# A long fp32 network, 256 tokens by 1024 features, on one core: another order at its beginning, at three boundaries and at its end, with GpSimd as a fourth arithmetic engine at the beginning

## The reference

```
def first_block(x, c, ctx, c_ctx, ...):        # sh, sc, ga = parts of silu(c) @ w_mod + b_mod
    hc = rmsnorm(ctx, g_mix) * (1 + csc1) + csh1
    hx = rmsnorm(x, g_mix) * (1 + sc1) + sh1
    x = x + ga1 * mlstm_mixer(hx, hc, ...)     # two directions, 4 heads, context as first state
    hx = rmsnorm(x, g_ffn) * (1 + sc2) + sh2
    x = x + ga2 * conv_glu(hx, ...)            # 1024 -> 2*2816 -> 1024
    return rmsnorm(x, g_final)

def sublayer(x, shift, scale, gate, g_pre, g_post, fn, w):
    h = rmsnorm(x, g_pre) * (1 + scale) + shift
    return x + w * gate * rmsnorm(fn(h), g_post)

def second_block(x, c, ...):                   # mods = silu(c) @ cond_w + cond_b
    x = sublayer(x, ..., swiglu_1, 0.5)        # stage f1
    x = sublayer(x, ..., gla_mixer, 1.0)       # stage gla, 4 heads
    x = sublayer(x, ..., swiglu_2, 0.5)        # stage f2
    k, v = mla_shared_kv(rmsnorm(x, kv_g) * (1 + kv_scale) + kv_shift)
    x = sublayer(x, ..., swiglu_3, 0.5)        # stage f3
    x = sublayer(x, ..., mla_mixer, 1.0)       # stage mla, 8 heads, causal softmax
    return sublayer(x, ..., swiglu_4, 0.5)     # stage f4
```

## Time and profile before

| | |
|---|---|
| three executions | 1379.90, 1382.67, 1385.39 us |
| their median | 1382.67 us |
| the profiled execution | 1383.82 us, of which 1382.0 us from its first to its last instruction |
| TensorE busy | 1354.5 us (98%) |
| DVE busy | 1121.2 us (81%) |
| ACT busy | 785.7 us (57%) |
| GpSimd busy | 1.4 us |
| DMA read | 335.5 MB, 244 GB/s over the span |

### The profile page before, as it was taken

The page is one execution under the profiler, slowest core; times in us unless marked ns, Lnnn a source line. Parts: engine busy times, 40 slices in busy tenths (PEclk is TensorE's granted clock), DMA queues, the critical chain, the costliest instruction groups (busy, mean ns, idle before and its releaser), DMA issues.

```text
span 1382.0 us, 19144 instructions
## 1 busy us (share of the span) xinstructions
PE 1354.5 (98%) x7488; PEld 1164.1 (84%) x7488; DVE 1121.2 (81%) x1652; ACT 785.7 (57%) x1153; POOL 1.4 (0%) x6
## 2 busy tenths in 40 slices
PE   7999999999999999999999999999999999999998
PEld 4988987888878888889878888888888998888886
DVE  7787787998988998779788888889888797796653
ACT  7623657666456555474475555476554646755552
POOL 0000000000000000000000000000000000000000
PEclk9999999999999999999999999999999999999999
DMA  9657445775958888767449778768879561575551
GB/s 379 264 197 281 152 138 182 279 259 198 332 201 305 303 278 320 288 244 271 154 175 328 284 281 327 278 246 319 294 288 379 197 226 64 199 259 183 183 187 57
DMA packets 63001, 337.77 MB, mean 244 GB/s; under 512 B 6960, under 2 KB 9392, under 8 KB 34752
## 3 DMA queue, kind: packets, MB, share of 16 engines
q1 hardware_dynamic: 62448, 335.35, 66.7%
q0 software_dynamic: 288, 1.05, 0.2%
q10 hardware_dynamic: 176, 0.16, 0.0%
HBM read 335.49 MB, written 1.05 MB: 244 GB/s over the span
## 4 chain that ended last, share of the span: by engine, by line
PE 89%; DVE 4%; ACT 3%; DMA 2%; issue 1%; SPq 0%; ACTq 0%; DVEq 0%
PE bank L313 87%; DMA XF<-xT 1%; DMA raw<-w_stream 1%; ACT rstd L665 1%; ACT T L760 1%; DVE wlo L309 1%; DVE X L854 1%; PE bank L635 1%; ACT whi L291 1%; PE bank L912 0%; DVE SGC L835 0%; PE bank L1042 0%; DVE XN L795 0%; PE bank L2370 0%; DVE wlo L282 0%
## 5 line engine op out<-in xcount | busy, mean ns | idle before, releaser
L313 PE MATMUL bank<-hh,whi 128*128 128x512 f32 (+1 forms) x2160 | 661.6, 369 | 4.0 <-DVE hh L558 3.4
L313 PE MATMUL bank<-hh,wlo 128*128 128x256 f32 x1896 | 525.7, 280 | 0.0
L309 DVE TENSOR_TENSOR wlo<-raw,whi 128x2048 fp32r<-128x2048 f32 x199 | 454.4, 2286 | 40.4 <-ACT whi L291 40.1
L313 PEld LDWEIGHTS bank<-hh,whi 128*128 128x128 f32 x2160 | 387.2, 190 | 79.7 <-DVE wlo L309 3.3
L291 ACT ACTIVATE whi<-raw 128x2048 fp32r<-128x2048 f32 x198 | 378.3, 1915 | 118.2 <-PE bank L313 84.5
L313 PEld LDWEIGHTS bank<-hh,wlo 128*128 128x128 f32 x1896 | 356.7, 189 | 0.0
L313 PE MATMUL bank<-whi,hid_hi 128*128 128x512 f32 x440 | 172.2, 391 | 0.0
L313 PE MATMUL bank<-whi,hid_lo 128*128 128x512 f32 x440 | 171.4, 390 | 0.0
L313 PE MATMUL bank<-wlo,hid_hi 128*128 128x512 f32 x440 | 171.3, 389 | 0.0
L937 DVE SCALAR_TENSOR_TENSOR mring<-mring,con 128x1024 f32<-128x1024 f32 x107 | 130.2, 1219 | 14.1 <-DMA mring<-m_stream 14.0
L1123 ACT ACTIVATE GU<-bank 128x512 f32<-128x512 f32 x100 | 59.1, 591 | 109.3 <-PE bank L313 109.3
(11 more groups left out here) (327 smaller groups left out, 1428.1 us busy)
## 6 DMA issues: line engine op xcount, KB each, us to landing
raw<-w_stream SPq DMA_DIRECT2D x217, 1024.0 KB, 5.1
mring<-m_stream SPq DMA_DIRECT2D x139, 512.0 KB, 5.0
cb<-m_stream SPq DMA_DIRECT2D x53, 512.0 KB, 5.2
raw<-w_stream SPq DMA_DIRECT2D x4, 512.0 KB, 7.3
con<-const_d SPq DMA_DIRECT2D x1, 1472.0 KB, 15.1
XF<-xT SPq DMA_DIRECT2D x1, 1024.0 KB, 13.2
XC<-ctxT SPq DMA_DIRECT2D x1, 1024.0 KB, 10.2
y<-OUT SPq DMA_DIRECT2D x4, 256.0 KB, 2.6
```

Of the source, the lines that this page charges most:

```text
L309: nc.vector.tensor_tensor(w_lo(c, 0, CW), raw[:, c % RAW_SLOTS], w_hi(c, 0, CW).bitcast(f32), ALU.subtract).then_inc(s_lo, 1)
L313: return nc.tensor.matmul(out, lhsT, rhs, start=start, stop=True, skip_group_check=True)
```

## The change

The change has five parts.

1. **Beginning.** DVE makes only the rest of the first half of chunk 8; GpSimd makes the second half's and both halves of chunk 9's (`pool_rest`, counted by `s_plo`, "first_rests_by_pool"), and then sums ACT's eight context squares in pairs (`pool_context_pairs`), so that the mean square is 2 float32 matmuls in place of 8. These stand between the two halves of keys(0,0). `pe_first_chunks` takes the products in another order. ACT splits chunk 9 in halves, one before the input tiles and one behind the second of them, and rounds chunks 10 and 11 before it squares the context.
2. **Turned tiles.** For t = 0 the tiles 4 and 5 go to bank 5 in place of bank 6, except at f3 and mla; only tile 6 waits.
3. **GLA.** SP issues chunk 92 ahead of the modulation rows; DVE takes a modulation row earlier, and the bias and coefficients of f2 before the last head.
4. **MLA.** Twelve matmuls of the output projection go before the last head's transposes and before its values.
5. **End.** For t = 1 TensorE turns the old X by 8 float32 matmuls with the identity, among the last output products, and adds the stage's output times the diagonal of rstd by 8 more (`pe_add_out`); ACT makes that diagonal, and the two updates of DVE are gone.

```diff
+        def dve_half_rest(dve, c, half):
+            units_ahead[c] = units[0]
+            a = half * HALF
+            dve.wait_ge((s_hih, s_hi)[half], c + 1)
+            nc.vector.tensor_tensor(w_lo(c, a, a + HALF), raw[:, c % RAW_SLOTS, a:a + HALF],
+                                    w_hi(c, a, a + HALF).bitcast(f32), ALU.subtract).then_inc((s_loh, s_lo)[half], 1)
...
+        s_plo = sem("first_rests_by_pool")
+        def pool_rest(pool, c, half):
+            a = half * HALF
+            pool.wait_ge((s_hih, s_hi)[half], c + 1)
+            nc.gpsimd.tensor_tensor(w_lo(c, a, a + HALF), raw[:, c % RAW_SLOTS, a:a + HALF],
+                                    w_hi(c, a, a + HALF).bitcast(f32), ALU.subtract).then_inc(s_plo, 1)
+        def pool_context_pairs(pool):
+            for n, j in enumerate((0, 4)):
+                pool.wait_ge(s_sq, DT + j + 4)
+                nc.gpsimd.tensor_tensor(SQF[:, j:j + 2], SQF[:, j:j + 2], SQF[:, j + 2:j + 4], ALU.add)\
+                    .then_inc(s_cpair, 1)
+            pool.wait_ge(s_cpair, 2)
+            nc.gpsimd.tensor_tensor(SQF[:, 0:2], SQF[:, 0:2], SQF[:, 4:6], ALU.add).then_inc(s_cpair, 1)
+        def pe_context_stat(pe):
+            pe.wait_ge(s_cpair, 3)
+            for j in range(2):
+                ins = mm(bank[7][:, SEQ:], ones, SQF[:, j], j == 0)
+            ins.then_inc(s_stat, 1)
         def pe_first_chunks(pe, u0, c):
...
+            def out(n, m):
+                return bank[4 + n][:, m * SEQ:(m + 1) * SEQ]
+            def high(k, n, m):
+                w = w_hi(c + n, (m * DT + k) * P, (m * DT + k + 1) * P)
+                mm(out(n, m), w, hhi[:, k], k == 0 and m == 0)
+                mm(out(n, m), w, hlo[:, k], False)
+            def low(k, n, m):
+                return mm(out(n, m), w_lo(c + n, (m * DT + k) * P, (m * DT + k + 1) * P), hhi[:, k], False)
             pe.wait_ge(s_hi, c + 1)
+            pe.wait_ge(s_loh, c + 1)
             for k in range(DT + 2):
                 if k < DT:
                     pe.wait_ge(s_h, u0 + k + 1)
-                    high(k, 0)
+                    high(k, 0, 0)
+                    low(k, 0, 0)
+                    high(k, 0, 1)
                 if k == 2:
-                    pe.wait_ge(s_hi, c + 2)
+                    pe.wait_ge(s_hih, c + 2)
                 if k >= 2:
...
+                    high(k - 2, 1, 0)
+            pe.wait_ge(s_hi, c + 2)
+            pe.wait_ge(s_plo, 2)
+            for k in range(DT):
+                high(k, 1, 1)
+                ins = low(k, 0, 1)
+                low(k, 1, 0)
+            ins.then_inc(s_pe, 1)
+            pe.wait_ge(s_plo, 3)
+            for k in range(DT):
+                ins = low(k, 1, 1)
+            ins.then_inc(s_pe, 1)
...
+        KEPT = ("f3", "mla")
+        def turned(pre, t, j):
+            b, n = (j // 2, j % 2) if t else (((6, 7, 6, 7) if pre in KEPT else (6, 7, 5, 6))[j // 2],
+                                              j // 4 * 2 + j % 2)
...
-                    if t == 0 and j == 4:
+                    if t == 0 and j == (4 if pre in KEPT else 6):
                         pe.wait_ge(s_t, MODULATED[pre] + 1)
-                    if t == 0 and j == 6:
+                    if t == 0 and j == 6 and pre in KEPT:
                         pe.wait_ge(s_vt, PRES.index(pre) + 1)
-                    nc.tensor.transpose(turned(t, j), XN[:, j * P:(j + 1) * P], ident).then_inc(s_tpn, 1)
+                    nc.tensor.transpose(turned(pre, t, j), XN[:, j * P:(j + 1) * P], ident).then_inc(s_tpn, 1)
...
+        s_dg = sem("last_rstd_diagonal")
+        def turned_out(t, j):
+            return bank[(6, 4)[t] + j // 4][:, (j % 4) * P:(j % 4 + 1) * P]
         def pe_turn_out(pe, t):
+            for j in range(DT):
+                if t == 0 and j % 4 == 0:
+                    pe.wait_ge(s_xu, XU["f4"] + j // 4 + 1)
+                if t == 0:
+                    nc.tensor.transpose(turned_out(t, j), X[:, t, j * P:(j + 1) * P], ident).then_inc(s_tpn, 1)
+                else:
+                    mm(turned_out(t, j), X[:, t, j * P:(j + 1) * P], ident, j % 4 == 0)
+        def pe_add_out(pe):
+            pe.wait_ge(s_dg, 1)
             for j in range(DT):
                 if j % 4 == 0:
-                    pe.wait_ge(s_xu, XU["f4"] + 2 * t + j // 4 + 1)
-                nc.tensor.transpose(bank[(6, 4)[t] + j // 4][:, (j % 4) * P:(j % 4 + 1) * P],
-                                    X[:, t, j * P:(j + 1) * P], ident).then_inc(s_tpn, 1)
+                    pe.wait_ge(s_tw, 4 * STAGES.index("f4") + 3 + j // 4)
+                mm(turned_out(1, j), TW[:, j // 4, (j % 4) * P:(j % 4 + 1) * P], XN[:, 0:P], False).then_inc(s_tpn, 1)
...
                 elif t:
+                    n = rn("post", "f4", 1)
+                    act.wait_ge(s_rr, n + 1)
+                    nc.scalar.activation(XN[:, 0:P], ident, ACT.Copy, scale=rr[:, n:n + 1]).then_inc(s_dg, 1)
                     act_turned_out(act, 1)
...
-                else:
+                elif t == 0 or stage != "f4":
                     dve_update(dve, stage, t)
...
-                pe_out_last(pe, c0 + FT + last, 2 * last, hid_hi, hid_lo, mid=lambda: pe_turn_out(pe, 0))
-                pe_turn_out(pe, 1)
+                pe_out_last(pe, c0 + FT + last, 2 * last, hid_hi, hid_lo, mid=lambda: pe_turn_out(pe, 0),
+                            second=lambda: pe_turn_out(pe, 1))
+                pe_add_out(pe)
...
-                pe_pair(pe, c + 3 + j, 4 + a % 3, *(((hhi, hlo), (chi, clo))[n]), n == 1)
+                pe_pair(pe, c + 3 + j, 4 + a % 3, *(((hhi, hlo), (chi, clo))[n]), n == 1,
+                        between=(lambda: pe_context_stat(pe)) if a == 2 else None)
...
+            dve_half_rest(dve, c, 0)
...
-            nc.vector.tensor_tensor(modc[:], pm[:, 1], cols[:, 0:FIRST_MODS], ALU.add)
             link(dve, nc.vector.tensor_tensor(mod[:, 0:FIRST_MODS], pm[:, 0], cols[:, 0:FIRST_MODS], ALU.add))
             dve_coef_pre(dve, 1, 8, col("g_mix", 0, 8))
             dve_modulate(dve, N_X1, cq(1), mcol(0), "x1", XF)
-            dve_split(dve, c)
-            dve_split(dve, c + 1)
+            link(dve, nc.vector.tensor_tensor(modc[:], pm[:, 1], cols[:, 0:FIRST_MODS], ALU.add))
             dve_coef_pre(dve, 0, 8, col("g_mix", 0, 8), modc)
-            dve_split(dve, c + 2)
+            dve_split(dve, c + 2, 3)
             dve_split(dve, c + 3)
...
             dve_split(dve, c + 14)
-            mods(dve, 2)
+            mods(dve, 3)
...
-            finish_head(3)
-            dve_split(dve, c + 16)
-            mods(dve, 1)
-            for j in range(17, 19):
-                dve_split(dve, c + j)
             bias(dve, "gla")
             dve_pre_coef(dve, "f2")
+            finish_head(3)
+            for j in range(16, 19):
+                dve_split(dve, c + j)
             dve_boundary(dve, "gla")
...
+            def out_first(g, t):
+                for half in range(2):
+                    if t == 0 and g == 0:
+                        pe.wait_ge(s_h, U["mla_y"] + 7 + half)
+                    ins = mm3w(out_bank(t, half), c, g * D + half * 512, tok(hhi, g, t), tok(hlo, g, t), g == 0)
+                return ins
...
+                    pe.wait_ge(s_lo, c + 1)
+                    pe.wait_ge(s_h, U["mla_y"] + 6)
+                    out_first(0, 1)
                 transposes(h)
                 if 0 < h < MLA_HEADS - 1:
                     values(h - 1)
+            out_first(1, 1)
             values(MLA_HEADS - 1)
...
+                ins = out_first(g, 0)
             ins.then_inc(s_pe, 1)
...
-                    if c in EARLY and c not in (C_GLA, C_FFN[2], C_KV + 1):
+                    if c in EARLY and c not in (C_FFN[2], C_KV + 1):
                         continue
...
-            pool.wait_ge(s_lo, C_LSTM + 1)
+            pool.wait_ge(s_hi, C_LSTM + 1)
             pool.dma_start(cb[:], c_row.partition_broadcast(P)).then_inc(s_in[4], 16)
+            pool_rest(pool, C_LSTM, 1)
+            for half in range(2):
+                pool_rest(pool, C_LSTM + 1, half)
+            pool_context_pairs(pool)
```

More of the change, by code:

```diff
@@ L274, in act_second_half @@
             nc.scalar.activation(w_hi(c, HALF, CW), raw[:, c % RAW_SLOTS, HALF:], ACT.Copy).then_inc(s_hi, 1)
[L276 to L283 removed]
+        def dve_half_rest(dve, c, half):
[4 more added lines that the diff above has]
+                                    w_hi(c, a, a + HALF).bitcast(f32), ALU.subtract).then_inc((s_loh, s_lo)[half], 1)
+        def dve_halves(dve, c):
+            for half in range(2):
+                dve_half_rest(dve, c, half)
         def act_split(act, c):
@@ L1304, in pe_lstm @@
             pe.wait_ge(s_mm0, 1)
-            pe_stat(pe, N_CTX)
             def keys(j, n):
```

40 lines of the change are left out of this document (8 added, 32 removed).

## The result

| | before | after |
|---|---|---|
| median | 1383.97 us (5 runs) | 1395.80 us (5 runs) |
| lowest and highest | 1379.90, 1385.61 | 1391.30, 1396.05 |
| profiled execution | 1383.82 us, span 1382.0 | 1395.80 us, span 1394.0 |

The ratio is 1.0075, 95% interval 1.0057 to 1.0094, so the change costs 10.4 us (7.9 to 13.0). I had forecast 1382.6 in a range of 1378.5 to 1389, with 0.11 on slower by more than 0.5%.

What follows compares the result with a forecast made beforehand. It took TensorE, busy 98% of the span, as the bound; -1.95 - 0.95 - 0.60 + 0.2 + 3.2 = -0.1 on 1383.82 gave 1383.7, or 1382.6 in the median's terms, range 1378.5 to 1389.

Steps and rivals of the forecast that it cites:

- GpSimd's rests are hidden: Beginning: GpSimd's half rests, 2.3 us each from about 34.2, and its sums end in time, with 2 us to spare.
- keys(1,0) -1.95: Beginning: keys(1,0) starts at 69.0 in place of 70.96 us, behind a new wait of 1.6.
- the first rival: Beginning: DVE and GpSimd take turns reading SBUF; keys(1,0) +1.15 for -1.95, time 1385.7 us; chance 0.36.
- The forecast's other half: Beginning: 16.2 us of DVE and ACT work from the mean square's end to keys(1,0), no instruction changed.
- GpSimd starts late: Beginning: GpSimd's first operation may be late; free up to 5.6 us, at 8 us costs 2.4 (1385.0); chance 0.12.
- Turned tiles, 0: Boundaries of f0 and f1: the first wait goes, the second grows by as much; gain 0.
- GLA, -0.95: gla's boundary: chunk 92's load goes ahead of two modulation rows, lands about 2 us earlier, removing TensorE's 0.95 wait.
- f2's -0.60: f2's boundary: a modulation unit done earlier, in an idle of DVE, removes TensorE's idle of 0.60 us.
- MLA, +0.2 (up to +1.2): MLA's last head: 0.99 of waits go, 0.8 and some 0.4 come; +0.2 us, between -0.9 and +1.2.
- The end, +3.2 with +1.4 as the other end: Last products: eight added turns cost 1.8 us; diagonal products at half clock give +3.2, at full clock +1.4.

Runs made afterwards that it cites:

- e9: Kernel before, with GpSimd adding spare SBUF tiles 48 times in stage f1, work that nothing needs; f1 is 36 us longer.
- e3: Kernel before with the changed beginning alone, GpSimd filling its three half rests with zeros (writes only); ratio 0.9994.
- e10: Kernel before with the changed beginning alone, GpSimd's three rests waiting for the end of DVE's scaling; ratio 1.0023.
- e1: Kernel before with the change's beginning (part 1) alone; ratio 1.0058.
- experiment 10: Kernel before with the GLA part alone, one execution; f2's boundary -0.8, gla's load 5.0 us with no wait.
- e8: Kernel before with e7's beginning, turned tiles, GLA part, old end, and only three MLA output products moved; median 1380.31 us, ratio 0.9971.
- e7: Kernel before with the changed beginning alone, DVE making the half rests and square sums in GpSimd's place; ratio 0.9992.

## Why the prediction was wrong, step by step

- **The step that failed: GpSimd's rests are hidden.** The forecast gave keys(1,0) -1.95; it is +5.1 to +5.5. GpSimd's speed (2.32 against 2.3) and its start were right, and TensorE never waits for GpSimd's rests. What was wrong is that its work costs the others nothing: while it reads SBUF, DVE's operations with two operands there stand still. The change's beginning with memsets in place of GpSimd's rests gives -1.3, the one without its arithmetic -1.6, so the rest of the sum was off by 0.4 to 0.6. The rule of the Trainium skill, "SBUF — State Buffer", section "Who interferes with whom", is that such a DVE instruction contends with a GpSimd one that reads and not with one that only writes. The traces agree: e9 and the change show the first half, e3 the second. I had it as the first rival with 0.36; no row spoke against it, and it should have been the forecast.
- **That rival's price was too low** by 3.9 to 4.3: it had +1.15. It let the two engines take turns and TensorE work meanwhile. In e9 and e10 they do take turns. But in the change and in e1 GpSimd's two first operations both went ahead of one waiting DVE step, at the one place where TensorE had no other work: 4.5 us of new idle (6.46 for 1.97). Why the step got no turn between them is not known. Half clock for 13.7 us in place of 3.4 came on top (3.4 to 6.8 in the traces with the old beginning). The forecast's other half held: the chain from the mean square to keys(1,0) took 16.3 (forecast 16.2), with the wait of 1.6 ahead of keys(1,0).
- **Rival "GpSimd starts late":** it didn't; 34.65 for 34.2.
- **Turned tiles, 0:** right. At f0's boundary the waits are 0.52 and 0.44, before 0.83 and 0.16.
- **GLA, -0.95:** wrong in its cause. I had the load go out ahead of two modulation rows and so land 2 us earlier; its issue does not move, because it waits for its slot (experiment 10). In the change's trace the load took 4.80 and the boundary gained 1.2, but e8, with the part, has 7.14 and the wait of 0.95, so that the gain came is luck as far as these traces tell. f2's -0.60 was right, -0.8 measured in all four traces with the part.
- **MLA, +0.2 (up to +1.2):** mis-sized, +2.4. I summed TensorE's waits and left out who queues behind the delayed values: DVE's last splits, and the rests behind these.
- **The end, +3.2 with +1.4 as the other end:** +1.5 (up to 2.1 against the old end at its fastest). The products with the diagonal ran at full clock in all three traces. The row that I chose as the nearest, eight turns at half clock, was a chance of that execution: the same turns ran at full clock in six of eleven traces. The terms as given (1.8, 2.19, 1.97, 1.9, and 1.8 or 3.5) also sum to +1.3 and +3.0, not to +1.4 and +3.2.
- **Sum.** What belongs to the change is 5.1 to 5.5 - 0.8 + 2.4 + 1.5 = 8.2 to 8.6 us against the first profile, inside the measured 7.9 to 13.0. Of the forecast's errors only the beginning's 7 us is large; the end, 1.7 too high, hid most of MLA's 2.2 too low by luck. The profiled execution's 12.0 has 3.8 more: +1.6 at f1's load, +1.9 and -1.9 of pace in f1 and f4, +3.5 at mla's load and the clock behind it, -1.2 at gla's.
- **Open.** The load ahead of mla's boundary took 7.0 to 7.7 in six of the seven traces with a changed beginning (all but e8), and 4.8 to 5.7 in all seven with the old one; f0 ran at its slower pace in five of those seven and in none of the others. So the late load and the slow f0 go with the changed beginning; by what path isn't known. If both the late load and the half clock behind it came in every execution, e7 would be some 2 us slower than before (-1.6 at the beginning, +3.9 at mla's load and the clock behind it) and not 1.1 faster (its interval ends at 1.5); but e7's profiled execution, at 1388.17, was one of its slowest. How often it happens is not settled, and with it what part of the 10.4 is more than the 8.2 to 8.6.
